# A hybrid recurrent and pooling block on eight cores: the first loads on one ring in a fixed order, the first recurrent weights cast on GpSimd

## The reference

```python
h = rms_norm(x, norm_mix_pre)
x_lru, g_lru, x_pool, gates = split(h @ w_in)            # 1024, 1024, 512, 2048 columns
x_lru = causal_depthwise_conv(x_lru, conv_w, conv_b)     # width 4
y_lru = rg_lru(x_lru, ...) * gelu(g_lru)                 # h_t = a_t h_{t-1} + u_t, a and u from two
                                                         # block-diagonal 64x64 gate maps
y_pool = multiscale_pool(x_pool, pool_w, pool_scale)     # trailing means over 2, 4, 8, 16, minus token
gate_a, gate_b = split(sigmoid(gates + b_gate))
m = (gate_a * (y_lru @ w_lru_up) + gate_b * (y_pool @ w_pool_up)) @ w_o
x = x + rms_norm(m, norm_mix_post)
f = square(relu(rms_norm(x, norm_mlp_pre) @ w_ff1)) @ w_ff2   # 4096 hidden channels
x = x + rms_norm(f, norm_mlp_post)
```

## Time and profile before

| | us |
|---|---|
| Median of three runs | 905.8 (904.81 to 906.87) |
| The profiled execution | 906.87 |
| Its slowest core (core 6), first to last instruction | 905.3 |
| Its fastest core (core 4) | 896.7 |
| PE busy on core 6 | 888.3 |
| DVE busy | 463.4 |
| ACT busy | 369.5 |
| POOL busy | 161.7 |

### The profile page before, as it was taken

How to read it: one execution, slowest core, us unless ns; L and a number is a source line. 1 busy time by engine, 2 the same in 40 slices (tenths; PEclk the granted TensorE clock), 3 DMA queues, 4 the chain that set the end, 5 groups by cost and what they waited for, 6 DMA issues and landing times.

```text
span 905.3 us, 13583 instructions; the slowest of 8 cores (896.7 to 905.3 us)
## 1 busy us (share of the span) xinstructions
PE 888.3 (98%) x4430; PEld 406.3 (45%) x4430; DVE 463.4 (51%) x666; ACT 369.5 (41%) x582; POOL 161.7 (18%) x304
## 2 busy tenths in 40 slices
PE   8999999999999999999999999999999999999997
PEld 6444434444444444444444444344444444444443
DVE  5559786984856866675554454111324334312122
ACT  5583967575473672442343334011113333311111
POOL 5222431302120011231222223100001111000000
PEclk9999999999999999999999999999999999999999
DMA  8953696136874297555598999911545544212121
GB/s 215 205 89 58 115 168 97 25 54 104 141 130 74 47 164 186 179 171 142 103 166 154 160 180 153 177 24 24 167 158 107 81 74 78 36 47 92 49 93 47
DMA packets 59830, 102.60 MB, mean 113 GB/s; under 512 B 29297, under 2 KB 29553, under 8 KB 59506
## 3 DMA queue, kind: packets, MB, share of 16 engines
q0 software_dynamic: 19872, 51.78, 36.8%
q1 hardware_dynamic: 39890, 49.96, 19.9%
HBM read 130.43 MB, written 16.78 MB: 163 GB/s over the span
## 4 chain that ended last, share of the span: by engine, by line
PE 89%; DMA 3%; issue 3%; DVE 3%; ACT 2%; SPq 0%; DVEq 0%; ACTq 0%
PE pp L543 63%; PE pp L912 24%; DMA big<-x 2%; PE pp L700 2%; ACT big L529 2%; DMA x1s<-big 1%; DVE big L809 1%; DVE big L764 0%; SPq L555 0%; PE pp L1075 0%; PE pp L589 0%; DVE big L814 0%; PE pp L783 0%; ACT L529 0%; DVE big L762 0%
## 5 line engine op out<-in xcount | busy, mean ns | idle before, releaser
L543 PE MATMUL pp<-big 128*128 128x512 bf16 x2880 | 627.9, 380 | 3.2 <-DVE hcar L767 2.1
L543 PEld LDWEIGHTS pp<-big 128*128 128x128 bf16 x2880 | 280.1, 98 | 346.7 <-issue 14.5
L529 ACT ACTIVATE big<-pp 128x512 f32<-128x512 f32 (+3 forms) x216 | 138.7, 644 | 401.7 <-PE pp L912 195.8
L912 PE MATMUL pp<-big 128*128 128x512 bf16 x1024 | 223.2, 381 | 2.2 <-DVE big L901 2.2
L901 DVE SCALAR_TENSOR_TENSOR big<-pp,big 128x512 bf16<-128x512 f32 x128 | 88.3, 690 | 134.6 <-ACT big L529 128.0
L912 PEld LDWEIGHTS pp<-big 128*128 128x128 bf16 x1024 | 100.5, 98 | 124.5 <-issue 4.8
L529 ACT ACTIVATE big<-pp,dv 128x512 f32<-128x512 f32 x128 | 81.4, 688 | 87.5 <-PE pp L543 61.6
L940 DVE TENSOR_TENSOR big<-pp,big 128x512 f32<-128x512 f32 x32 | 22.1, 692 | 172.7 <-ACT big L529 164.5
L555 POOL DMA_DIRECT2D big<-wff x80 | 44.0, 551 | 222.0 <-PE pp L543 202.9
L529 ACT ACTIVATE big<-big 128x1024 bf16<-128x1024 f32 (+1 forms) x64 | 66.0, 1050 | 23.2 <-DVE big L875 12.6
L838 DVE SCALAR_TENSOR_TENSOR big<-big,pp 128x512 bf16<-128x512 f32 (+1 forms) x64 | 42.9, 683 | 30.4 <-PE pp L543 22.2
(11 more groups left out here) (65 smaller groups left out, 341.8 us busy)
## 6 DMA issues: line engine op xcount, KB each, us to landing
big<-x SPq DMA_DIRECT2D x32, 512.0 KB, 6.5
big<-wff POOLq DMA_DIRECT2D x64, 256.0 KB, 4.3
big<-wmrga POOLq DMA_DIRECT2D x16, 512.0 KB, 7.3
x1s<-big SPq DMA_DIRECT2D x16, 512.0 KB, 3.9
big<-wff POOLq DMA_DIRECT2D x16, 512.0 KB, 8.5
big<-x1s SPq DMA_DIRECT2D x16, 512.0 KB, 4.3
out<-big SPq DMA_DIRECT2D x32, 256.0 KB, 2.0
big<-wlru POOLq DMA_DIRECT2D x14, 512.0 KB, 8.4
```

Of the source, the lines that this page charges most:

```text
L529: return e.activation(out=o, in_=i, func=func, **kw)
L543: ins = e.matmul(P.bank(tile, k)[:, width], lhsT=lt, rhs=rh, start=(i == 0), stop=(i == len(g) - 1))
L912: ins = e.matmul(P.bank(v, k0), lhsT=hid[k][:, TS], rhs=wff2[nh][k // 4][:, k % 4, :], start=(k == 0), stop=(k == 31))
```

## The change

All first loads go on SP's queue, back to back, in one order written out by hand (`FRONT`): the gain row, x0, the identity, the column vectors, x1 to x3, the four pieces of the first pair's weights with x4 and x5 between them, x6, x7, and the gate maps last. The weight pieces and `wab` are loaded as fp32 into staging memory. POOL casts the four pieces to bf16; DVE casts `wab` as it places it. `x` has eight buffers for its first eight tiles. The diagonal matrices of the first pair are made by DVE. The first pair's products run on 256 tokens at a time, so each needs two tiles of `x` and not four. POOL's own first loads now wait for x5, w11 or x7 (`XG`, `gate`). The last two tiles of stage A, and the last two of stage E's second half, are transposed on PE (`TRP`). The planner's numbers for the order of the stages are new (`PC`, `PD2`, `PD1`, `PWO`, `PE0`, `PF1`, `W2`, `GEARLY`), and so is its estimate of when an SP load begins.

```diff
-    PC = ((-10.0, 13.83), (424.04, 26.15))
-    PD2 = ((39.35, 81.22), (566.54, 90.4))
-    PD1 = (1065.62, 93.96)
-    PWO = 1125.97
-    PE0 = (1193.64, 24.22)
+    PC = ((-10.0, 13.83), (424.04, 23.62))
+    PD2 = ((39.53, 81.22), (566.54, 53.56))
+    PD1 = (1065.62, 86.13)
+    PWO = 1056.11
+    PE0 = (1147.69, 24.22)
-    W2 = (-4.03, 4.69, 14.95, 3.57)
-    XG = 4
-    GEARLY = 1.54
+    W2 = (-11.76, 4.69, 14.95, 3.92)
+    NRA = 8
+    XG = (14, 11, 14, 12, 12)
+    GEARLY = 1.44
-    XW = (2, 4, 5, 2)
-    XX = (1, 2, 3, 3)
-    PWAB = -1701.42
+    FRONT = ('g1', 'x0', 'id', 'cv', 'x1', 'x2', 'x3', 'w00', 'w10', 'x4', 'w01', 'x5', 'w11', 'x6', 'x7', 'wab')
+    TRP = (2, 0, 2)
-    xinA = [carve(o, 4) for o in (80, 84, 56, 60, 190.1875, 194.25)]
+    xinA = [carve(o, 4) for o in (80, 84, 56, 60, 190.1875, 194.25, 174.125, 178.125)]
-    wabs = carve(136, 2, BF16, V3, b=64)
+    wabs = carve(136, 4, F32, V3, b=64)
+    wst = {(0, 0): carve(104, 4), (1, 0): carve(108, 4), (0, 1): carve(128, 4), (1, 1): carve(132, 4)}
+    def front_load(name, dst, src, nbytes):
+        front[name] = P.add("sp", lambda e: e.dma_start(out=dst, in_=src), writes=[dst], dma="f_" + name,
+                            prio=-3000 + FRONT.index(name), nbytes=nbytes, work=nbytes / 312.0)
+    for (n, k), t in wst.items():
+        front_load("w%d%d" % (n, k), t, WLRU[n][:, 1024 * k:1024 * k + 1024], 524288)
+    front_load("wab", wabs, WAB.rearrange(V3, b=64), 524288)
...
-    def gate(pr, lead):
+    def gate(pr, lead, x=0):
         k = int((pr - lead) // 100)
-        return [bmm[k]] if 0 <= k < len(bmm) else x_loads[XG:XG + 1] if k < 0 else []
+        return bmm[max(0, k):k + 1] + [front[FRONT[XG[x]]]] * (k < 2)
...
-        for k, (pr, after) in enumerate(((-1990.0, x_loads[XW[0]:XW[0] + 1]), (-1700.0, x_loads[XW[1]:XW[1] + 1]))):
-            load("pool", "wlru%d_%d" % (n, k), w[:, 8 * k:8 * k + 8, :],
-                 WLRU[c][:, 1024 * k:1024 * k + 1024].rearrange(V3, b=128), 524288, prio=pr + n, after=after)
+        for k in range(2):
+            casts.append(P.add("pool", lambda e, k=k: e.tensor_copy(out=w[:, 8 * k:8 * k + 8, :], in_=wst[n, k].rearrange(V3, b=128)),
+                  reads=[wst[n, k]], writes=[w[:, 8 * k:8 * k + 8, :]], ns=1150.0, prio=-1800 + n + 2 * k))
...
+    def mm_b(w, Q, v, prio, quarters):
+        step = 256 if quarters else 512
+        for o in range(0, 512, step):
+            S = slice(Q.start + o, Q.start + o + step)
+            i = mm([[(w[:, k, :], hT[:, k, S]) for k in range(8)]], [w, hT[:, :, S]], [(v, 0, slice(o, o + step))], prio,
+                   n=step)
+        return i
...
+        if tl >= 8 - TRP[1 + h]:
+            transposes(hb, tt, pr, "act")
+        else:
+            transposes_dma(hb, tt, pr)
```

More of the change, by code:

```diff
@@ L685, in fn @@
             return ins
-        P.add("pool", fn, reads=[identb[:], cvt[:, C_CW:C_CW + 32]], writes=[dst], ns=2400.0,
-              prio=-900 if n < 2 else 100.0 * n - 120)
+        if n < 2:
+            dve(fn, [identb[:], cvt[:, C_CW:C_CW + 32]], [dst], ns=500.0, prio=-2000)
+        else:
+            P.add("pool", fn, reads=[identb[:], cvt[:, C_CW:C_CW + 32]], writes=[dst], ns=2400.0, prio=100.0 * n - 120,
+                  after=casts if n < 4 else ())
     LO, HI = slice(0, 64), slice(64, 128)
@@ L720, in stage_B @@
                 vx = Ps(1)
-                i = mm([[(w[:, k, :], hT[:, k, Q]) for k in range(8)]], [w[:, 0:8, :], hT[:, :, Q]], [(vx, 0, ALLW)], pu + 20 * m)
+                i = mm_b(w[:, 0:8, :], Q, vx, pu + 20 * m, n == 0)
                 if r == 0:
@@ L731, in stage_B @@
                 vg = Ps(1)
-                mm([[(w[:, 8 + k, :], hT[:, k, Q]) for k in range(8)]], [w[:, 8:16, :], hT[:, :, Q]], [(vg, 0, ALLW)], pu + 20 * m + 1)
+                mm_b(w[:, 8:16, :], Q, vg, pu + 20 * m + 1, n == 0)
                 act(g[:, R], lambda vg=vg: P.bank(vg), AF.Gelu_apprx_tanh, reads=[vg], prio=pu + 20 * m + 1)
@@ L774, in fold_pool @@
     def fold_pool(g, pr):
-        load("pool", "wpt", wpt, WPT[g], 524288, prio=pr - 100, after=gate(pr, 150))
+        load("pool", "wpt", wpt, WPT[g], 524288, prio=pr - 100, after=gate(pr, 150, 1))
         v = Ps(2)
@@ L882, in stage_E @@
             [xin, rs2, gA], [hb], n=1024, ns=1290.0, prio=pr)
-        transposes_dma(hb, tt, pr)
+        if tl >= 8 - TRP[1 + h]:
+            transposes(hb, tt, pr, "act")
+        else:
+            transposes_dma(hb, tt, pr)
     nf1 = [0]
@@ L984, in build_nc @@
     load_lru(1, 1)
-    load("pool", "wab", wabs, WAB.rearrange(V3, b=64), 524288, prio=PWAB, after=x_loads[XW[2]:XW[2] + 1])
     for p in range(2):
         wabp = wab[64 * p:64 * p + 64, :, 64 * p:64 * p + 64]
-        dve(lambda e, p=p, wabp=wabp: e.tensor_copy(out=wabp, in_=wabs[64 * p:64 * p + 64]), [wabs], [wab], ns=420.0,
+        dve(lambda e, p=p, wabp=wabp: e.tensor_copy(out=wabp, in_=wabs[64 * p:64 * p + 64]), [wabs], [wab], ns=690.0,
             prio=-999.4)
-    load("pool", "poolw", poolw, POOLW.rearrange(V3, b=128), 262144, prio=-1600, after=x_loads[XW[3]:XW[3] + 1])
+    load("pool", "poolw", poolw, POOLW.rearrange(V3, b=128), 262144, prio=-1600, after=[front[FRONT[XG[4]]]])
     F = P.filler
```

36 lines of the change are left out of this document (18 added, 18 removed).

## The result

The changed kernel takes 919.7 us (median of 4 runs, 919.4 to 920.9), the kernel before, run beside it, 905.3 (903.6 to 906.9): a ratio of 1.016, 95% interval 1.014 to 1.018. The forecast was 898.5, its range 891.5 to 907. The profiled run took 919.42 us. In this document runs over 1.5% above the fastest of their kernel, most of them with one half of the chip at a lower clock and at 960 us or more, count neither in the medians nor in the ratios (in e7 two, at 920.4 and 920.7 us, are among them).

A forecast was written before the change was run, and what follows sets the result against it. PE was busy 888.3 of 905.3 us, leaving the start, two PE waits and the lowered clock after them to win; 906.87 - 7 + 0.2 + 1.9 - 3 = 899.0, from the median 897.9, stated as 898.5, range 891.5 to 907.

The forecast's parts named there:

- Transposes on PE: Last tiles of stages A and E: 32 transposes at 0.061 us add 1.9 us on PE; four leave SP's queue.
- Everything else: New order of D and E stages: 0, with 0 to 4 us against it for one wait and its clock.
- The first pair: Start: the pair's work ends at 37 us in place of 45.15 on core 6; gain taken as 7 us.
- x7 in hT 32.4: Start: last of the first eight tiles ready at 26.3 + 1 + 5.1 = 32.4 us.
- DVE takes the start's gain back: Rival, 73 to 123 us: DVE's chain begins no sooner, PE waits, 2 of the 7 us kept; 904 us, chance 0.14.
- The wait at 571 us: PE's wait for DVE behind the write of x1s: goes as the write gets 2 us shorter; booked at 3 us.
- The wait at 123 us: PE's 2.1 us wait for DVE, a scan ahead of a needed cast: let stand, no gain booked.
- Casts: Start: POOL's four casts of the first pair's weight pieces take 1.5 us each; 0 booked for the end of the start.
- Arrivals: Start: landings such as x6 at 24.6, w11 at 23.0, wab at 28.0 us; last weight piece 13 us sooner.
- 256-token products: First pair: 64 more instructions, weight loading stays hidden; adds 0.2 us.
- a new wait: Rival, somewhere in the new order: 4 us with its clock, beside a start of only 3; 908 us, chance 0.06.

The follow-up runs named there:

- e7: e3 with the stage numbers of the kernel before put back, so the new start alone: 915.4 us, ratio 1.007.
- e1: Changed kernel with tiles 14 and 15 of stage A transposed by DMA again: 919.3 us, ratio 1.014.
- e3: Changed kernel with no tile after the eighth transposed on PE, in stage A or E, all by DMA: 919.5 us, ratio 1.014.
- e12: Transfers alone, nothing computed: loads and DMA transposes on one core at a time, then all; longest landing with one core at work 12.4 to 33.7 us.
- e18: Changed kernel with each DMA transpose issued only when the one before has landed: 912.2 us, ratio 1.001.
- e10: Changed kernel, stage A's later tiles on PE, none of E's, roots of tiles 4 to 7 on POOL ahead of second pair's diagonals: 919.8 us, ratio 1.014.
- e8: e3 with the first pair's products on 512 tokens as before: 927.4 us, ratio 1.021.
- e11: Kernel before with only the first pair's products changed to 256 tokens: 919.7 us, ratio 1.013.
- e15: e3 with each DMA transpose issued only when the one before has landed: 914.4 us, ratio 1.004.
- e17: e7 with each DMA transpose issued only when the one before has landed: 910.1 us, ratio 0.998.
- e13: Transfers alone in five kinds of block; longest landings 13.3 to 33.5 us whole, 5.7 to 6.8 without weights, 5.6 to 14.1 one at a time.

## Why the prediction was wrong

The step that cost most is the price that the forecast put on a DMA transpose. *Transposes on PE* (1.9 us) asked only how many of them leave the queue, and let one landing time of 10.3 us stand for those that stay; *Everything else* had at most 4 us for a wait and its clock. Their own cost on PE is of the size forecast. What decided was that PE's fixed order hangs on DMA transposes that land after 11.7 us at most on one core and after 24.3 on another. It was worth 14.4 us on the slowest core, and some 2 of clock. That tile 14 stood on PE is not the point: with it back on DMA (e1, e3) PE waits on slow cores for something else in the same stretch, and the time stays. The earlier trace rows had two transposes at 10.3 us beside six loads, where e12 has 3.3 us for one without loads: the sign was there, without a row to compare it with. e18 takes the slow landings away (9.6 us at most) and keeps the rest of the change: the ratio is 1.001.

*The first pair* (gain 7) failed in its term "x7 in hT 32.4". It was written by 38.8 on core 7, 11.9 us after its landing at 26.8: the row of 5.1 us for a tile was that of a tile among tiles, while tile 7 stands among the pair's GeLUs and their table loads, ahead of which the forecast put nothing. Of the gain nothing came: in the first 50 us PE spent 17.3 to 18.4 us on dummy products and idling, on the eight cores (before 15.7 to 18.0). And it would not have been kept: in e10 tile 7 came 4 us sooner and the time rose. The rival "DVE takes the start's gain back" had a mechanism of that kind; I gave it 0.14.

*The wait at 571 us* (3 us) stayed: 1.3 to 3.1 us on the eight cores, 0.9 to 2.4 before. The step that failed is that the write of x1s gets 2 us shorter by the new W2: over the cores the last write took 9.0 to 10.8 us, 9.0 to 10.3 before (the 9.20 above and the 10.07 of the earlier trace rows are single cores).

*The wait at 123 us* stays: right (1.8 us). *Casts* right: 1.03 to 1.92 us on core 7 for 1.5, the mean 1.5 there. The Trainium skill (GPSIMD Engine Reference, section 3.1) gave an estimated 1.5 as its best case; 19 of the 32 casts on the eight cores took 1.03 to 1.07 us, so the trace is faster than that best case. *Arrivals* right: x6 near 25.3 us for 24.6, w11 at 23.4 for 23.0, wab at 29.5 for 28.0.

*256-token products* (0.2 us) hold as the price of the instructions. That the new front is 8 us slower without them (e8, 927.4 us, against e3, 919.5), and that alone they make the kernel before slower by 1.3% (e11), I put down to the order that the planner then makes (in e11 that of PE, DVE, ACT and POOL all change), which I had not counted as a cost of this edit; no run takes the two apart.

*Everything else* (0, with 0 to 4 against it): the middle core of e15 stands 3 us behind that of e17, which has the old numbers, and the longer wait at 571 us is most of it. So the new numbers, which were to take that wait away, made it longer (e3 against e7).

The rival *a new wait* (0.06) had the right kind of mechanism with 4 us for a price; the range ended where it did because I bounded a wait by the waits that the trace already had.

Still open: why a transpose in flight with another beside a second queue of loads goes slow in one block and not in the next, and thus why the kernel before, with nearly the same order of transfers from 95 to 130 us, mostly escapes. That another order tips it is shown (e11); which property of an order does is not. Of the 7 us on the middle cores 4 are left in e18 (906.5 against 902.5): by estimate 1.9 of them are the transposes on PE and 1 the longer wait at 571 us; the rest has no account.

## What to carry over

Where an engine's fixed order hangs on a DMA, take the spread of that DMA over cores and over its neighbours, not its median, as the price. Try one DMA transpose in flight where loads run on another queue: here one dependency took 7.5 us off a kernel whose slow cores changed from run to run, some 14 by the ratios; on the kernel before it changed nothing that could be measured. A start that ends sooner is worth only what the next shared chain doesn't already wait for; trace that chain to its end before booking it.

## What the hardware showed

In e12 a DMA transpose of 128x1024 bf16 lands 3.3 us after its issue, 1.3 us behind the one before, alike on all cores, as long as nothing is loaded; 1.3 us is also what each issue takes on SP. With loads beside it, on its own and on a second queue, it took up to 39.8 us there, and the loads of wlru up to 25.6 in place of 5 to 6. e13 puts it down to the second queue: 5.7 to 6.8 us for the longest of eight without it, 13.3 to 33.5 with it. The Trainium skill (Advanced Engine Details and Errata, section X-Bar Transpose (TRN2)) has transpose DMAs as fast as regular ones. No run here shows that: by themselves they move 0.25 MB in 1.3 us, where a plain load moves 0.5 MB in 1.66 us (*Arrivals* in the prediction), and beside loads they are slower still.
